# Two norms and the first weight blocks moved into neighbouring stages, and latent attention's scores as rounded products over 128 rows

## The reference, cut to what matters

```python
# first block, after the two mixers
x = x + jnp.concatenate([o_dn, o_dsa], axis=-1) @ w_out[l]
hx = rmsnorm(x, g_xattn[l])
mn = rmsnorm(mem, g_mem[l])                       # 256 rows of memory
... cross attention of hx over mn: w_xq, w_xkv ...
x = x + ox @ w_xo[l]
x = x + (jax.nn.silu(hf @ w_gate[l]) * (hf @ w_up[l])) @ w_down[l]

# second block, two layers
fq, fk, fv, ff, fg, q_lat, kv_lat, k_r, mg = jnp.split(h @ w_in[l], splits, axis=-1)
y_fox = fox_attention(fq, fk, fv, log_f) * silu(fg)             # 8 heads of 64
q  = rms_norm(q_lat, q_norm_g[l]) @ w_uq[l]                     # 256 -> 8 heads of 64+32
kv = rms_norm(kv_lat, kv_norm_g[l]) @ w_ukv[l]                  # 128 -> 8 heads of 64+64
q_rope, k_rope = apply_rope(q_rope), apply_rope(k_r)
s = (q_nope . k_nope + q_rope . k_rope) * (64+32)**-0.5          # fp32 scores, block-causal
y_mla = softmax(s) @ v * silu(mg)
x = x + gate * (concat([y_fox, y_mla]) @ w_out[l])
```

## Time and profile before

| | us |
|---|---|
| three timed runs | 3907.14, 3910.28, 3915.74 |
| their median | 3910.28 |
| the profiled execution, whole | 3912.11 |
| its span, first to last instruction | 3910.3 |

### The profile page before, as it was taken

The page is one execution under the profiler, slowest core; times in us unless marked ns, Lnnn a source line. Parts: engine busy times, 40 slices in busy tenths (PEclk is TensorE's granted clock), DMA queues, the critical chain, the costliest instruction groups (busy, mean ns, idle before and its releaser), DMA issues. The chain is left out here.

```text
span 3910.3 us, 46909 instructions
## 1 busy us (share of the span) xinstructions
PE 3399.1 (87%) x18212; PEld 2640.3 (68%) x18228; DVE 1947.1 (50%) x3220; ACT 1182.1 (30%) x2182; POOL 1094.7 (28%) x578
## 2 busy tenths in 40 slices
PE   5688799589778987999999978999897889998978
PEld 4367566479667866788787857766565677765657
DVE  3599677755435433745455471233454412334553
ACT  3354355434312222100000030333453112333540
POOL 2123000045226524534353433211102332211012
PEclk9799899689888998999999989999899999998999
DMA  3111100000202112312222112100002211000011
GB/s 108 28 28 38 30 4 3 1 7 2 70 29 74 54 38 72 114 64 96 65 86 75 54 27 87 29 26 6 16 2 72 79 39 39 22 12 16 2 68 67
DMA packets 228786, 171.04 MB, mean 44 GB/s; under 512 B 42224, under 2 KB 215840, under 8 KB 227840
## 3 DMA queue, kind: packets, MB, share of 16 engines
q1 hardware_dynamic: 225440, 167.81, 14.0%
q10 hardware_dynamic: 3168, 0.81, 0.1%
HBM read 151.66 MB, written 16.93 MB: 43 GB/s over the span
## 5 line engine op out<-in xcount | busy, mean ns | idle before, releaser
L842 DVE TENSOR_TENSOR I-13378act_f<-I-13377act_g,I-13384p_u 128x512 f32<-128x512 f32 x44 | 28.3, 684 | 239.1 <-PE I-13384p_u L273 239.1
L1010 DVE SCALAR_TENSOR_TENSOR y_T<-y_T 128x1024 f32<-128x1024 f32 x48 | 139.7, 2961 | 5.9 <-DMA y_T<-in_w_ada 5.9
L828 ACT ACTIVATE I-13377act_g<-I-13383p_g 128x1024 f32<-128x1024 f32 x22 | 22.6, 1028 | 389.5 <-PE I-13383p_g L273 389.5
L1572 DVE TENSOR_TENSOR I-22323S<-I-22323S,c_causal 128x256 f32<-128x256 f32 x32 | 13.8, 432 | 228.9 <-PE I-22323S L1510 228.9
L1572 DVE TENSOR_TENSOR I-16043S<-I-16043S,c_causal 128x256 f32<-128x256 f32 x32 | 13.8, 432 | 219.3 <-PE I-16043S L1510 219.3
L269 PE MATMUL I-13383p_g<-hf_hi,I-13359w_hi 128*128 128x512 f32 x352 | 109.5, 392 | 5.1 <-POOL hf_lo L495 5.0
L271 PE MATMUL I-13383p_g<-hf_lo,I-13359w_hi 128*128 128x512 f32 x352 | 109.1, 391 | 0.0
L273 PE MATMUL I-13383p_g<-hf_hi,I-13361w_lo 128*128 128x512 f32 x352 | 108.8, 390 | 0.0
L269 PE MATMUL I-13384p_u<-hf_hi,I-13360w_hi 128*128 128x512 f32 x352 | 108.4, 389 | 0.0
L273 PE MATMUL I-13384p_u<-hf_hi,I-13362w_lo 128*128 128x512 f32 x352 | 108.4, 389 | 0.0
L271 PE MATMUL I-13384p_u<-hf_lo,I-13360w_hi 128*128 128x512 f32 x352 | 108.3, 389 | 0.0
(11 more groups left out here) (1413 smaller groups left out, 10284.4 us busy)
## 6 DMA issues: line engine op xcount, KB each, us to landing
y_T<-in_w_ada SPq DMA_DIRECT2D x48, 512.0 KB, 3.5
saved_x<-x_T SPq DMA_DIRECT2D x3, 4096.0 KB, 11.8
x_T<-saved_x SPq DMA_DIRECT2D x3, 4096.0 KB, 15.3
I-13357w_raw<-in_w_gate SPq DMA_DIRECT2D x22, 512.0 KB, 4.6
I-13358w_raw<-in_w_up SPq DMA_DIRECT2D x22, 512.0 KB, 4.1
I-13371d_raw<-in_w_down SPq DMA_DIRECT2D x11, 512.0 KB, 4.6
I-13372d_raw<-in_w_down SPq DMA_DIRECT2D x11, 512.0 KB, 4.9
I-941w_raw<-in_w_in SPq DMA_DIRECT2D x8, 512.0 KB, 3.8
```

The costliest lines, as they stand in the source:

```text
L828: nc.scalar.activation(act_g[:, :], flat(p_g), ACT.Silu).then_inc(gated, 1)
L842: nc.vector.tensor_tensor(act_f[:, cols], act_g[:, cols], p_u[:, h, :], ALU.mult).then_inc(product, 1)
L1010: self.nc.vector.scalar_tensor_tensor(out=self.raw[s], in0=self.raw[s], scalar=1.0, in1=self.c_row, op0=ALU.mult, op1=ALU.mult, accum_out= ...
L1572: self.nc.vector.tensor_tensor(diag, diag, tiled(self.mask, 2), ALU.add).then_inc(self.masked, 1)
```

## The change

Seven edits, with no change to what is computed but the rounding of the mla scores:

1. **Memory norm.** `load_stage` and `norm_stage` for the memory go away. A class `MemoryNorm` does the same work inside the first `project_stage`, in steps behind its blocks: two groups of transposes on PE behind blocks 0 and 1, squares, sums (behind block 3), spread (behind 5), scale and rounding behind block 6.
2. **Latent norms.** Both `norm_stage`s of the second block go away. Their work stands in the last pair of `fox_stage`: squares on ACT at t = 0 and 1, sums on PE at t = 2, root on ACT and inverse and diagonals on DVE at t = 3, four spreads on PE and four scalings on DVE at t = 4 to 7, roundings on ACT and rests on DVE one and two units later.
3. **Fillers of fox.** The latents' six halves move from the last pair into pairs 0 to 2, two in each; these now have a filler at every t, and the last pair has none.
4. **mla scores.** Query and key of a head, 64 plain and 64 rotary rows, stand in one tile of 128 rows, split into `hi` and `lo`. A stretch of up to 512 keys is three rounded matmuls a head. Query weights come as one block a head. Each query half is copied by ACT and rotated by DVE into a scratch, rounded by ACT and its rest made by DVE; each key half is rounded and its rest made for either head; the rotary key is rounded and split once for each of two slots.
5. **First weight block ahead.** `cross_stage` and `mla_stage` load and split the first block of the next `project_stage` (`w_xo`, `w_out_2`) at the end of their SP and POOL queues.
6. **POOL held back.** In `blocks_stage` (with a norm), `ffn_stage` and `gates_stage` POOL waits for the norm's diagonal before it splits the first block; in the first two `norm.pool` comes between the first and the second block. A `project_stage` with a block made ahead waits with its next block until six rests are made.
7. `project_stage`'s loops are written out.

```diff
 # project_stage
+                for j in range(KD):
+                    if j == 1 and ahead is not None:
+                        pool.wait_ge(y_split.sem, KD - 2)
+                    sw.split(pool, j // 2, j % 2, P)
...
+                    sw.multiply(pe, j // 2, j % 2, P, ..., norm=y_split if j == 0 else None)
+                    if side is not None:
+                        side.pe(pe, j)
 # blocks_stage
+                if norm:
+                    pool.wait_ge(norm.ir.diag_ready, 1)
                 for b, (cols, _, _) in enumerate(blocks):
                     sw.split(pool, 0, b, cols)
-                    if norm and b == 1:
+                    if norm and b == 0:
                         norm.pool(pool)
 # fox_stage, PE
-                    if t in HALF_AT:
-                        m = 6 * (i + 1) + HALF_AT[t]
+                    if i < LAST:
+                        m = filler(i, t)
                         pe.wait_ge(hb.out, m)
                         hb.multiply(pe, m, KD, half_of(m), hi, lo)
+                    elif t == 2:
+                        latent_sums(pe)
+                    elif t >= 4:
+                        latent_spread(pe, t - 4)
 # fox_stage, DVE
+                    if i == LAST:
+                        if t == 1:
+                            latent_add(dve)
+                        elif t == 2:
+                            latent_var(dve)
+                        elif t == 3:
+                            latent_invert(dve)
+                        elif t >= 4:
+                            latent_scale(dve, t - 4)
+                        if t >= 6:
+                            latent_rest(dve, t - 6)
 # mla_stage
-            return [(lambda h, t: ph.q[i % 2][rows(h), t * P:(t + 1) * P], lambda h, a, b: ph.k[i % 2][rows(h), a:b]),
-                    (lambda h, t: q_rope[i % 2][rows(h), t * P:(t + 1) * P], lambda h, a, b: key_rope[rows(h), a:b])]
+            return [(tile(q_hi_of), cols(k_hi_of)), (tile(q_lo_of), cols(k_hi_of)), (tile(q_hi_of), cols(k_lo_of))]
 # mla_stage, ACT: keep(m)
-                    nc.scalar.activation(dst[:, part], half_of(m), ACT.Copy, scale=scale if b == BK else 1.0).then_inc(hb.out, 1)
+                    elif b == BK:
+                        for h in range(2):
+                            rows = nope_rows[h]
+                            nc.scalar.activation(k_hi_of[i % 2][h][rows, part], half_of(m)[rows, :], ACT.Copy, scale=scale).then_inc(k_rounded, 1)
+                    else:
+                        h = b - BQ0
+                        wait(act, hb.out, m - 1)
+                        nc.scalar.activation(turning[m % 2][nope_rows[h], :], half_of(m)[nope_rows[h], :], ACT.Copy).then_inc(q_copied, 1)
+                        act.wait_ge(q_copied, q_halves(m) + 1)
+                        act.wait_ge(q_turned, q_halves(m) + 1)
+                        nc.scalar.activation(q_hi_of[i % 2][h][:, part], turning[m % 2], ACT.Copy).then_inc(q_rounded, 1)
...
+                    if u == 0:
+                        round_key(1)
 # mla_stage, DVE: rest(m), behind the scaling of each unit; its end sets hb.out
+                        dve.wait_ge(k_rounded, 2 * (k_halves(m) + 1))
+                        for h in range(2):
+                            last = nc.vector.scalar_tensor_tensor(out=k_lo_of[i % 2][h][rows, part], in0=half_of(m)[rows, :], ...)
...
+                        dve.wait_ge(q_rounded, q_halves(m) + 1)
+                        last = nc.vector.tensor_tensor(q_lo_of[i % 2][h][:, part], turning[m % 2], q_hi_of[i % 2][h][:, part].bitcast(F32), ALU.subtract)
```

More of the change, by code:

```diff
@@ L248, in split @@
         s, n = b % 2, (kt or self.kt) * cols
-        pool.wait_ge(self.loaded[s], 16 * self.dmas.after(i, b))
+        if self.is_made(i, b):
+            self.nc.gpsimd.memset(self.mark[:, 0:1], 0.0).then_inc(self.rounded[s], 1)
+            self.nc.gpsimd.memset(self.mark[:, 1:2], 0.0).then_inc(self.ready[s], 1)
+            return
+        not_loaded = self.dmas.w[0] if self.made and s == 0 else 0
+        pool.wait_ge(self.loaded[s], 16 * (self.dmas.after(i, b) - not_loaded))
         wait(pool, self.used[s], self.steps.before(i, b))
@@ L684, in project_stage @@
         squares = SquareSums(st, nc, x_T, ssq)
+        side = memory and MemoryNorm(st, nc, const, *memory)
         with nc.Block() as block:
@@ L737, in _ @@
-                squares.dve(dve, KD // 2 - 1, 1)
+                for j in range(KD):
+                    dve.wait_ge(sw.used[j % 2], j // 2 + 1)
+                    x_n, sums = x_T[:, j, :], acc[j % 2][:, :, :].rearrange("p h n -> p (h n)")
+                    if gate is None:
+                        nc.vector.tensor_tensor(x_n, x_n, sums, ALU.add).then_inc(added[j % 2], 1)
+                    else:
+                        nc.vector.scalar_tensor_tensor(out=x_n, in0=sums, scalar=gate[:, j:j + 1], in1=x_n, op0=ALU.mult, op1=ALU.add).then_inc(added[j % 2], 1)
+                    if j > 0:
+                        squares.dve(dve, (j - 1) // 2, (j - 1) % 2)
+                    if side is not None:
+                        side.dve(dve, j)
@@ new lines, in fox_stage, with latent_sums @@
+        parts_done = [2, 4, 5, 6]
+        cut = lambda h: slice(h * BANK, (h + 1) * BANK)
+        def latent_sums(pe):
+            pe.wait_ge(l_added, 1)
+            pe.wait_ge(l_squared, 3)
+            pe.wait_ge(hb.out, N_HALVES)
+            for g, squares in ((0, sq[0]), (1, sq_kv)):
+                for t in range(NT):
+                    last = nc.tensor.matmul(ph.half[:, g * NT + t:g * NT + t + 1], squares[:, t * P:(t + 1) * P], const["c_ones"][:, 0:1], start=True, stop=True)
+            last.then_inc(l_summed, 1)
@@ new lines, in latent_spread, with latent_squares @@
+        def latent_spread(pe, n):
+            g, h = PARTS[n]
+            pe.wait_ge(l_diag, g + 1)
+            pe.wait_ge(l_var_set, 2)
+            if n > 0:
+                pe.wait_ge(l_scaled, parts_done[n - 1])
+            nc.tensor.matmul(ph.half[:, :], const["c_ones"][:, :], diag[g][:, 4 * h:4 * h + 4, :].rearrange("p t n -> p (t n)"), start=True, stop=True).then_inc(l_spread, 1)
+        def latent_squares(act, tiles):
+            act.wait_ge(hb.out, N_HALVES)
+            for k in tiles:
+                nc.scalar.activation(sq[k] if k < KQ else sq_kv, lat[:, k, :], ACT.Square).then_inc(l_squared, 1)
```

355 lines of the change are left out of this document (259 added, 96 removed).

## The result

The changed kernel takes 3886.95 us (median of four runs, 3881.97 to 3887.43) against 3913.01 for the kernel before in the same comparison: ratio 0.9931, 95% interval 0.9917 to 0.9945. It is faster by 26 us. The forecast was 3842 with a range of 3798 to 3876, so the sign was right, the gain was 38% of the one forecast, and the time lies outside the range.

What follows compares the result with a forecast made beforehand. Prediction: mostly PE's own work bounds the kernel (busy 87%), the rest is waits. Terms -22.5 - 50.8 + 27 + 10 - 22 - 9.5 = -67.8, less 1.8, take 3912.1 to 3842 us; range 3798 to 3876.

Steps and rivals of the forecast that it cites:

- Memory norm: Memory's load and norm stretch of 25.8 us goes, 3.3 of PE work returns between blocks: -22.5 us.
- Latent norms: Second block's two latent norm stretches of 25.4 us each go: -50.8 us; what returns is counted in fox.
- Fox, the moved halves: Fox pairs 0 to 2 gain two halves each, 10.9 us less 1.3 covered: three pairs cost 29 us.
- Fox, the last pair: Fox's last pair loses six halves, takes the norm's steps and falls to its chain: 59.7 us instead of 75.1.
- mla: Both mla stages: cheaper PE scores against more ACT and DVE work, +5 us a layer, +10 in all.
- the replay: mla's order replayed unit by unit: scores start 4.0 us later, pair 0 loses 3.2, pairs 1 and 2 end +0.2 each.
- the rival that they hide: In mla rests hide beside exps and masks, so PE's 15.3 us a layer counts: 3802 us, 13%.
- Score matmuls: mla scores: six rounded passes, 1.36 us, replace four fp32 ones, 1.72, per 512 keys of two heads: 15.3 us a layer.
- First block ahead: Three project stages: PE starts 7.4 us sooner in each with the first weight block ready: -22 us.
- POOL held back: Blocks stage and layer 0's gates: DVE's steps run without POOL's split beside them, ffn and layer 1 unchanged: -9.5 us.
- the chains cost more: Rival: mla's pairs held at every filler, or latents' work on fox's last pair by 20 us: 3870 to 3880, 12%.
- the clock: Rival: longer waits in mla's first units and fox's last pair get 1.2 GHz instead of 2.4; half gives about 4020, 3%.

Runs made afterwards that it cites:

- The early matmuls: The changed kernel with eight useless 512-wide matmuls added in fox's last pair at t = 0 and at t = 1: 3874.54 us, ratio 0.9906.

## Why the prediction missed

What the change saves came mostly as forecast. What failed is what it costs: one step in fox and two in mla.

- **Memory norm**: right, -23.1 for -22.5.
- **Latent norms**: right, the stretches went as a whole.
- **Fox, the moved halves**: right. Pairs 1 and 2 took 79.7 us as forecast, pair 0 75.5. The three cost 27.8 us where the sum had 29.
- **Fox, the last pair**: 65.2 and 67.8 for 59.7. The step that failed is "the sums on PE (32 of them at 0.11 = 3.5, of which 2.8 shows)". 0.11 was the price at full clock, worked out from a row at half clock; they took 7.1, and scores and transposes behind them took nearly twice their time too. With the clock at 0.86 they take 3.8, so the price was right and the clock was not. The mechanism was in the prediction only as a rival that had to be large enough to turn the sign, at 3%. It belonged into the sum as a term: the row from which the sums were priced stands in a stage at 0.61, and the change moves those very sums. What the earlier trace rows couldn't tell is that PE would be busy nearly all the time there and still be at 0.53. The early matmuls, which took 3.7 and 6.1 us off, show it. A further 1.4 and 0.7 us lie ahead of the first scores (44.6 us for 43.2 and 43.9); the run with the fox stage of before has 44.8 and 44.4 there, so they are not the moved work's.
- **mla**: +16.8 and +17.3 for +5. By its own terms: prologue 5.7 (forecast 4.0), pair 0 4.5 (3.2), pairs 1 and 2 without the collision 2.6 each (0.2 each), last pair -1.8 (-3.5), POOL's block 3.4 (1). Two steps failed. "POOL's block made ahead adds about 1" has no working and leaves out what POOL stops on DVE, although show one and the same DVE instruction at 1.2 to 3.4 us and the prediction itself puts that down to POOL under the first block. It cost 3.4 us a layer. And the replay ("end +0.2 each") was wrong for pairs 1 and 2; it gave back the later masks to shorter later units, but t = 4 to 7 are bound by PE and can't give back time that PE spent waiting: in pair 1 t = 0 to 3 became 4.9 us longer and t = 4 to 7 only 2.4 shorter. That the rests are what holds was right, and the rival that they hide was wrong: without them the stage is 16 to 18 us shorter. The replay also priced PE's work at full clock, and that is a part of the miss: 1.9 us in the first half of pair 1 by the run without rests.
- **Score matmuls**: right in price, too large in sum. They stand 0.23 apart at 512 columns, and t = 4 to 7 gained 2.4 us a pair, some 10 a layer. The sum had 15.3. A stretch of 128 keys costs 0.11 a matmul as one of 256 does, so in unit 4 it even became dearer, 0.61 us (2829.14 to 2829.75) where fp32 took 0.54, and of the 0.10 one end stayed. The 0.10 of the earlier trace rows is gone at the end of a group (from the last score at 2829.64 to the first transpose at 2829.75 there is just the score's own 0.11) and still there at its start, behind values of 64 columns. The rule of the Trainium skill (TensorEngine Tiling (Array Packing), Key Properties), a drain at a change of tiling mode, fits both. The other reading, a change of number type, doesn't: where the rounded half follows the fp32 transposes on the same tile, four transposes of 0.11 from 2830.21 on and one matmul of 0.23 give 2830.88, and the half's second matmul starts at 2830.89. Rows of PE's timeline, unit 4 of pair 1:

```profile
2827.64 0.50 PE L1600 MATMUL I-19127S<-I-19160kh,I-19152qh 128*128 128x512 f32 x1
2827.98 0.40 PE L1600 MATMUL I-19127S<-I-19161kh,I-19153qh 128*128 128x512 f32 x1
2828.22 0.39 PE L1600 MATMUL I-19127S<-I-19160kh,I-19156ql 128*128 128x512 f32 x1
...
2829.64 0.28 PE L1600 MATMUL I-19127S<-I-19165kl,I-19153qh 128*128 128x128 f32 x1
2829.75 0.62 PE L1611 MATMUL I-19128PT<-c_ident,I-19133probs 128*128 128x128 f32 x4
```

- **First block ahead**: -20.3 for -22 in the stages where it is used; its making was the error named above.
- **POOL held back**: -4.7 for -9.5. The seven scalings came to 9.2 us and not 8.6. The other 1.6 of the blocks stage, the 2.2 of ffn and the 1.3 of layer 1's gates are of the size by which these stages vary without an edit, so whether the terms for them were wrong stays open.

Of the rivals, "the chains cost more" (12%) and the clock were both partly true at once. The range left out their sum: the 24 us missed in mla alone give 3866, the 11 in fox alone 3853, both within it; together with the 8 of the other rows they pass 3876.

## What to carry to other kernels

When work that filled a matrix engine's gaps moves elsewhere, price what stays behind at the lower clock level too, and look at what short instructions replace it. Here a wait of 1.68 us and a row of one-column matmuls were followed by 26 us at a clock of 0.53 to 0.56 in layer 0. A few useless large matmuls ahead of such a stretch, and the same ones behind its start as a control, tell in two runs whether this is so. Work given to an idle GpSimd wasn't free here, since a VectorE instruction on the critical path ran at that time and took 3.87 us instead of 1.42; tie such work to a point at which that engine waits anyway. And a cheaper matmul whose operands need one more step in a loop back to PE can cost more than it saves: here 10 us a layer of PE against 16 to 18 for the rests.
